# The second block's projections on one core: where the recurrence's second states, the gates' transposes, the PSUM turn and eight stores stand

## What is computed

```python
proj = h @ w_in
(dn_q, dn_k, dn_v, dn_z, dn_a, dn_b, gl_q, gl_k, gl_v, gl_g, gl_r) = jnp.split(proj, offsets, axis=-1)
log_a = -jnp.exp(dn_a_log) * jax.nn.softplus(dn_a + dn_dt_bias)
log_alpha = jax.nn.log_sigmoid(gl_r @ gla_w_gate2 + gla_b_gate) / GLA_TAU
def step(S, inp):
    qd_i, kd_i, v_i, oi_i, gl_i = inp
    o = jnp.einsum('bhcd,bhde->bhce', qd_i, S) + oi_i
    S = S * gl_i[..., :, None] + jnp.einsum('bhcd,bhce->bhde', kd_i, v_i)
    return S, o
```

## Time and profile before

| | us |
|---|---|
| median of three runs | 3502.37 |
| lowest, highest | 3501.4, 3503.48 |
| the profiled execution | 3501.52 |
| its span in the profile | 3499.8 |
| TensorE busy | 3388.2 (97%) |
| VectorE busy | 1972.0 (56%) |
| ScalarE busy | 1338.8 (38%) |
| stage of the change, about | 2057 to 2477 |

### The profile page before, as it was taken

How to read it: one execution, slowest core, us unless ns; L and a number is a source line. 1 busy time by engine, 2 the same in 40 slices (tenths; PEclk the granted TensorE clock), 3 DMA queues, 4 the chain that set the end, 5 groups by cost and what they waited for, 6 DMA issues and landing times.

```text
span 3499.8 us, 39552 instructions
## 1 busy us (share of the span) xinstructions
PE 3388.2 (97%) x16122; PEld 2757.0 (79%) x16122; DVE 1972.0 (56%) x2389; ACT 1338.8 (38%) x1883; POOL 458.9 (13%) x325
## 2 busy tenths in 40 slices
PE   8999999999999899999999999999799989999998
PEld 6788888877876688888888867787698778888886
DVE  8454462234655344787762364444676688888235
ACT  4232212434255524333321266343445454444214
POOL 0000000000010001444420110000000045554000
PEclk9999999999999999999999999999999999999999
DMA  3313241112400124233266212121104323334722
GB/s 120 74 52 115 103 166 58 55 49 91 171 25 22 34 85 133 85 120 108 109 231 250 73 52 103 66 91 56 66 1 151 102 79 109 115 114 156 308 91 83
DMA packets 116118, 355.92 MB, mean 102 GB/s; under 512 B 16200, under 2 KB 26184, under 8 KB 115920
## 3 DMA queue, kind: packets, MB, share of 16 engines
q1 hardware_dynamic: 113824, 353.05, 28.7%
q10 hardware_dynamic: 2112, 0.33, 0.1%
HBM read 269.20 MB, written 82.95 MB: 101 GB/s over the span
## 4 chain that ended last, share of the span: by engine, by line
PE 85%; DVE 7%; ACT 6%; issue 1%; DMA 0%; ACTq 0%; SPq 0%; DVEq 0%
PE PS L491 42%; PE PS L2456 21%; PE PS L474 9%; PE PS L3800 1%; PE PS L3812 1%; PE PS L1923 1%; PE PS L2931 1%; PE PS L1945 1%; PE PS L509 1%; PE PS L1615 1%; PE PS L989 1%; ACT dS L1671 1%; ACT whi L431 0%; PE PS L3805 0%; PE PS L3030 0%
## 5 line engine op out<-in xcount | busy, mean ns | idle before, releaser
L436 DVE TENSOR_TENSOR wlo<-raw,whi 128x1024 fp32r<-128x1024 f32 (+3 forms) x393 | 500.1, 1273 | 415.4 <-ACT whi L431 412.5
L431 ACT CAST whi<-raw 128x1024 fp32r<-128x1024 f32 (+3 forms) x393 | 372.9, 949 | 748.1 <-PE PS L491 341.0
L491 PE MATMUL PS<-xhi,whi 128*128 128x512 f32 x1872 | 603.2, 403 | 16.4 <-DVE sbVt L2141 6.3
L491 PE MATMUL PS<-xlo,whi 128*128 128x512 f32 x1872 | 581.0, 392 | 0.0
L491 PE MATMUL PS<-xhi,wlo 128*128 128x512 f32 x1872 | 579.6, 391 | 0.0
L491 PEld LDWEIGHTS PS<-xhi,whi 128*128 128x128 f32 x1872 | 346.6, 189 | 102.8 <-issue 13.7
L491 PEld LDWEIGHTS PS<-xlo,whi 128*128 128x128 f32 x1872 | 353.4, 189 | 75.7
L491 PEld LDWEIGHTS PS<-xhi,wlo 128*128 128x128 f32 x1872 | 353.2, 189 | 75.6
L2456 PE MATMUL PS<-tf,whi 128*128 128x512 f32 x936 | 288.1, 389 | 1.7 <-DVE wlo L436 1.7
L2456 PE MATMUL PS<-xhi,whi 128*128 128x512 f32 x624 | 243.9, 391 | 7.2 <-DVE xlo L2441 5.6
L2456 PE MATMUL PS<-xlo,whi 128*128 128x512 f32 x624 | 243.5, 390 | 0.0
(11 more groups left out here) (558 smaller groups left out, 5584.9 us busy)
## 6 DMA issues: line engine op xcount, KB each, us to landing
raw<-in_w_up SPq DMA_DIRECT2D x88, 512.0 KB, 3.3
hid<-hs SPq DMA_DIRECT2D x88, 512.0 KB, 3.6
raw<-in_w_in SPq DMA_DIRECT2D x67, 512.0 KB, 3.3
slot<-hid SPq DMA_DIRECT2D x56, 512.0 KB, 6.7
adr<-in_w_ada SPq DMA_DIRECT2D x48, 512.0 KB, 4.7
raw<-in_w_down SPq DMA_DIRECT2D x48, 512.0 KB, 3.6
raw<-in_w_gate SPq DMA_DIRECT2D x32, 512.0 KB, 3.3
merged<-hid SPq DMA_DIRECT2D x16, 512.0 KB, 13.2
```

The costliest lines, as they stand in the source:

```text
L431: act.e.copy(whis[i % RING][:, ks, :], raws[i % RING][:, ks, :]).then_inc(*give("w_hi", i))
L436: dve.e.tensor_tensor(wlos[i % RING][:, ks, :], raws[i % RING][:, ks, :], whis[i % RING][:, ks, :].bitcast(F32), ALU.subtract).then_inc(*g ...
L491: ins = pe.e.matmul(ps[:, h * 512:(h + 1) * 512], w[s][:, k, :], x[:, h * 512:(h + 1) * 512], start=(at == 0 and n == 0), stop=(at == kt - ...
```

## The change

It moves work and changes no instruction of the computation. Four parts:

- TensorE asks for the pairs of the first three products one by one, each ahead of its own first half, and no longer for all three at the start.
- `gates` and the recurrence's gate step of pair 0 no longer stand ahead of product 2's second half, but behind three of its eight blocks.
- In slots 9 and 23, st1 stands behind six of the product's eight blocks. The list of pairs is turned by one before the product and by one more before st1: product 9 still takes product 8's pair, `states(12, 3)` still that of `states(4, 4)`, and the outputs of the next slot take the pair of product 9 (of 23), and product 10 that of the transposes.
- The eight scalings and their stores stand four in slot 1, two in slot 3 and two in slot 4 (`PUTS`).

```diff
--- before.py
+++ after.py
@@ -3231,9 +3231,11 @@
         G_STEPS = ("gate", "sum", "exp", "kd", "kT", "at", "st0", "st1", "o", "sq", "root", "d", "parts")
         G_FROM = (2, 16)
 
-        def gla_steps(eng, gla, slot):
+        ST1_IN = {start + G_STEPS.index("st1"): hp for hp, start in enumerate(G_FROM)}
+
+        def gla_steps(eng, gla, slot, skip=()):
             for hp in range(2):
-                if 0 <= slot - G_FROM[hp] < len(G_STEPS):
+                if 0 <= slot - G_FROM[hp] < len(G_STEPS) and G_STEPS[slot - G_FROM[hp]] not in skip:
                     gla(eng, hp, G_STEPS[slot - G_FROM[hp]])
 
         def away_landed(eng, hp):
@@ -3434,6 +3436,8 @@
                     dve.wait_ge("ox_hi", f, 0)
                     lo_of(dve, GLO[hp][hh], GO[hp][hh], GHI[hp][hh], "ox_lo", f, 0)
 
+        PUTS = {1: 4, 3: 2, 4: 2}
+
 
         PARKED = [FT[0][0], FT[0][1], FT[1][0], FT[1][1], VT[0], VT[1]]
         PARK_AT = {8: (0,), 9: (1,), 10: (4,), 14: (2,), 15: (3, 5)}
@@ -3460,11 +3464,10 @@
                     for name, dst in (("upper", upper), ("mG", mG), ("mS", mS), ("mT", mT), ("lev", lev)):
                         sp.e.dma_start(dst, A["c_" + name]).then_inc(*land("c_" + name))
                 else:
-                    for _ in range(4):
-                        k = next(puts, None)
-                        if k is not None:
-                            sp.wait_ge("put", k)
-                            sp.e.dma_start(spill[:, k, :], X2[:, k, :]).then_inc(*land(f"lane{k}", "spill"))
+                    for _ in range(PUTS.get(slot, 0)):
+                        k = next(puts)
+                        sp.wait_ge("put", k)
+                        sp.e.dma_start(spill[:, k, :], X2[:, k, :]).then_inc(*land(f"lane{k}", "spill"))
                 if kind == "z":
                     sp.wait_ge("z_out", ft)
                     sp.e.dma_start(spill[:, 8 + ft - 12, :], work_tile("z", ft)).then_inc(*land(f"away{ft - 12}", 0))
@@ -3529,24 +3532,37 @@
             UNTIL = {"small": "sm", "q": "raw2", "k": "raw2", "v": "raw2", "z": "z_out", "gq": "gqk", "gk": "gqk", "gv": "v_raw", "gz": "z_out"}
 
             until = [("sm",) if kind == "small" else (UNTIL[kind], ft) for kind, ft in PROJ]
-            first = [opened(pe, dense, "w_in2", PROJ[n][1], until[n]) for n in range(3)]
+            first = []
             norm = ln0_second_pe(pe)
-            for i, ps in first:
-                for _ in half_steps(pe, i, ps, HX1, 0, done=False):
+            for n in range(3):
+                first.append(opened(pe, dense, "w_in2", PROJ[n][1], until[n]))
+                for _ in half_steps(pe, *first[n], HX1, 0, done=False):
                     next(norm, None)
             for _ in norm:
                 pass
             drive([half_steps(pe, i, ps, HX1, 1) for i, ps in first[:2]])
             for slot, (kind, ft) in enumerate(PROJ):
-                gla_steps(pe, gla_pe, slot)
+                gla_steps(pe, gla_pe, slot, ("st1",) if slot > 2 else ("gate",))
                 if slot == 2:
-                    drive([half_steps(pe, i, ps, HX1, 1) for i, ps in first[2:]])
+                    steps = half_steps(pe, *first[2], HX1, 1)
+                    for _ in range(3):
+                        next(steps)
+                    gates()
+                    gla_pe(pe, 0, "gate")
+                    drive([steps])
+                elif slot in ST1_IN:
+
+                    dense.append(dense.pop(0))
+                    steps = product_steps(pe, dense, "w_in2", ft, HX, until[slot])
+                    for _ in range(6):
+                        next(steps)
+                    dense.append(dense.pop(0))
+                    gla_pe(pe, ST1_IN[slot], "st1")
+                    drive([steps])
                 elif slot > 2:
                     product(pe, dense, "w_in2", ft, HX, until[slot])
                 projected()
-                if kind == "small":
-                    later.append(gates)
-                elif kind in ("q", "k"):
+                if kind in ("q", "k"):
                     later.append(lambda ft=ft: unit(ft))
                 elif kind in ("v", "gv"):
                     later.append(lambda ft=ft: token(ft))
@@ -3564,12 +3580,12 @@
                     act.wait_ge("ln0_lo", k, 1)
                     act.e.activation(X2[:, k, :], X2[:, k, :], ACT.Identity, scale=ga[:, k:k + 1], bias=ba[:, k:k + 1]).then_inc(*give("put", k))
 
-            def projected():
+            def projected(slot):
                 todo = later[:]
                 del later[:]
                 for f in todo:
                     f()
-                for _ in range(4):
+                for _ in range(PUTS.get(slot, 0)):
                     put()
 
             def gates():
@@ -3598,7 +3614,7 @@
                 work_free(act, "raw", ft)
                 act.wait_ge("prod", i)
                 act.e.copy(work_tile("raw", ft), psum.of(i)).then_inc(*give("raw2", ft))
-                projected()
+                projected(slot)
                 act.wait_ge("conv", ft)
                 act.e.activation(proj_dst(ft), proj_dst(ft), ACT.Silu).then_inc(*give("conv_silu", ft))
 
```

## The result

| | before | after |
|---|---|---|
| median, us | 3502.93 (4 runs) | 3485.10 (4 runs, 3484.77 to 3489.17) |
| profiled execution | 3501.52 | 3484.9 |
| its span | 3499.8 | 3483.2 |

The ratio is 0.995, its 95% interval 0.9939 to 0.9962: 17.8 us, 0.5%, faster. Forecast were 3484.5 and a gain of 17.9. In a later job the changed kernel gave 3485.68 beside 3502.63 (5 and 9 runs; ratio 0.9951, 0.9938 to 0.9963). The sum was nearly right, but two of its terms were not: the stage itself gained 15.0 us, and 1.6 us of the profiled gain lie outside it. That the two errors were made up for was luck.

A forecast was written before the change was run, and what follows sets the result against it. TensorE, busy 97% of the span, was taken to bound the kernel; 2.8 + 7.0 + 8.1 = 17.9 us off 3501.5 gives 3483.6, as a median 3484.5 us. Range 3482.3 to 3490.5, chance 0.83.

The forecast's parts named there:

- Start: First products of the stage: one pair request per product lets matmuls start earlier; 2.8 us gained, bounds 1.4 to 2.8.
- all the new waits are below 2.02, so the sum has none: Clock step: new waits of 1.9, 0.9, twice 0.45 and 1.25 us leave TensorE's clock high, so no loss is counted.
- The bound of 1.4: Start of the stage: the gain if the new 1.9 us wait for block 6 leaves the clock low.
- rival (1): Low clock falls at one or two new waits, likeliest the start or before the outputs: 3486 to 3490 us; chance 0.25.
- Gates, stores and product 4: Slots 2 to 4: product 4 starts 4.3 us earlier and runs at the high clock; 7.0 us in sum.
- The cover of 1.2 us: Slots 3 to 6: DVE's products end at 2142.5, TensorE wants them at 2143.7; cover shrinks from 6.7 us.
- rival (2): ScalarE's and DVE's chain of slots 3 to 6 becomes late, TensorE waits in slot 6: 3487.5 to 3491 us; chance 0.10.
- Rival (4): Slower than before: scanm, issued behind four stores and a weight load, lands 30 us late: 3511 us; chance 0.02.
- a term of 1.6: Gates inside product 2: the wait before their transposes goes, 1.6 us, with nothing late in its place.
- Second states: Second states inside products 9 and 23: 4.6 us gained in the first place, 3.5 in the second, sum 8.1.
- The new wait of the outputs: Output matmuls after products 9 and 23 wait 1.25 us for ScalarE's copy to free the product's pair.
- rival (3): Short waits bring the clock down everywhere, at the start, product 4, products 9 and 23: 3494.6 us; chance 0.04.

The follow-up runs named there:

- start_alone: The kernel before, with only the PSUM pairs of the first three products asked for one by one: 3496.58 us beside 3503.38.
- after_again: The changed kernel itself, unaltered, run again in a later job beside its variants: 3485.68 us, ratio 0.9951 to the kernel before.
- gates_alone: The kernel before, with only the gates' transposes and gate products set inside product 2: 3503.66 us beside 3503.38.
- behind_8: The changed kernel without the second PSUM turn, and with the last states behind all eight blocks of the product, not six: 3487.98 us.
- no_turn: The changed kernel with no turn of the PSUM list around products 9 and 23: 3493.22 us beside 3501.09.

## Why the prediction was right, and where its steps were not

**Start: forecast 2.8, measured 1.3.** The path was right: first matmul behind the stage before, a wait for L2703, 1.73 us for block 6 (forecast 1.9). Where the clock stays high it gives the 2.8 (start_alone). In the changed kernel product 1's second half ends 36.3 us behind L2703, before 37.6, which is 1.3 earlier. The step that failed is "all the new waits are below 2.02, so the sum has none": behind this wait the clock fell, in seven of eight traces that have it, and takes 1.5 us back. The bound of 1.4 that stood beside the 2.8 was the likelier value. The row on which the step stood, the 2.02 us wait of the earlier trace rows with the clock at 1.00 behind it, is itself the rarer case: in 10 of 14 traces the low clock follows that same wait (after_again). The cause of the loss was rival (1)'s, at the place it named first, though the time did not come out in rival (1)'s 3486 to 3490.

**Gates, stores and product 4: forecast 7.0, measured 7.1.** Product 4 starts 56.49 us behind L2703 and not 62.26, 5.8 earlier; with the start's 1.3 taken off that is 4.5 (forecast 4.3). It takes 11.19 and not 13.85. The cover of 1.2 us on ScalarE's and DVE's chain, on which rival (2) hung, came out as 1.5. Rival (4) hung on scanm; it was no longer waited for at all. That the gates gain nothing alone was not said: the prediction wrote them as a term of 1.6 that was "inside" the 4.3, and gates_alone shows that it is only there when ScalarE's scalings are out of the way.

**Second states: forecast 4.6 + 3.5, measured 3.7 + 2.9.** The new wait of the outputs was found beforehand, with its cause, but sized 1.25 us. In the first place the silu starts 0.55 us behind the product's end (2199.19 to 2199.74) and not 0.2, and TensorE stands 1.56. The other half microsecond is the product itself: its pieces of 8.42, 1.93 and 2.89 us are 0.5 more than the forecast 12.75 with switches. Why the silu starts later in the first place than in the second (0.2) stays open. Neither the 1.2 nor the 1.56 us waits were followed by a low clock. The prediction does not say how much of this part is the clock; by start_alone it is 2.7 of the first place's 3.7.

**What lay outside.** In the profiled executions, L2703 to the first L3786 of the next stage (L3770 before, at 2477.43) takes 401.08 us and not 416.11: 15.0 gained where 17.9 were forecast. The span fell by 16.6: 0.35 ahead of the stage, 1.2 behind it, neither worked out. Most of both comes from where the low clock fell in code that the change leaves alone. Ahead of the stage it fell behind the wait at 115.74 us before and not after, where that wait was 0.93 us; behind L1923 it fell after and not before; 0.35 is what remained. Behind the stage the granted clock over 50 us was 0.90 before (2502 to 2552) and 0.97 after (2487 to 2537), which puts the second trace 1.5 us ahead; 0.3 of it is lost again later. Such gains are not the change's to promise: in the traces of the other kernels the part behind the stage ran from 3.0 us shorter to 1.7 longer than before. The forecast met the median to 0.6 us by luck: these parts, and the 0.7 us by which the medians fell more than the profiled executions, made up for two terms that were both 1.5 too large.

**Rule and row.** The prediction sets beside its clock step what the Trainium skill says of idle spells between groups of matmuls that cycle through PSUM (TensorE: Matmul & The Clock Gate, A second HAM failure mode: psum-queue depth-cycling), and says that it speaks for "the last rival"; the rival that it speaks for is (3). The traces agree with it in part: the waits of 0.74 to 1.56 us for a pair, before product 4 and before the outputs, left the clock high in every trace, which is against rival (3), while behind the longer ones, 1.97 us at the old place of the states and 2.25 and 4.19 us in behind_8 and no_turn, it fell in all places but one. The one of 1.73 was for data and not for a pair.

## What to carry to other kernels

Moving waiting work into a product pays only with the right buffer turn: here the same place with no turn gained nothing, with two turns 3.7 us and with one 5.5 (2.7 of each is the low clock that no longer followed), so write down the last three requests of the round and who reads each pair before choosing. Gains in a row of queues don't add: take each edit alone as well as together, since one may be worth nothing until another clears the queue behind it. Read gains of a few microseconds between two fixed events of the trace, and count a new idle spell at both clock levels. One row in which a wait left the clock high is no bound: look at the same place in a second trace.

## What the runs showed of the hardware

A wait of 1.72 to 1.73 us at the same place was followed by the low TensorE clock in seven traces (granted clock 0.66 to 0.75 from 2065 to 2070) and by the full clock in one. A wait of 1.97 to 2.02 us at L1923, in code that is the same in every kernel, was followed by it in ten traces and not in four. So the length of one wait doesn't decide it, and the same code can fall or not. A wait of 4.19 us was followed by it in both places of no_turn, one of 2.25 in both of behind_8, and none of ten waits of 1.20 to 1.56 us before the outputs was. One such stretch cost 1.5 us at the start of the stage, where seven matmuls ran slow, 2.66 us in product 4 (13.85 instead of 11.19) and 2.7 us in slots 8 and 9 (27.36 instead of 24.68).
